# Squares of each head summed over the channels: one f32 matmul replaced by two fp32r matmuls on a rounded part and a remainder

## What is computed

```
def _head_rms(h, w):                                   # A and C
    hn = h * lax.rsqrt(jnp.mean(jnp.square(h), -1, keepdims=True) + LN_EPS)
def _head_ln(h, w):                                    # B
    hc = h - jnp.mean(h, -1, keepdims=True)
    hn = hc * lax.rsqrt(jnp.mean(jnp.square(hc), -1, keepdims=True) + LN_EPS)
```

## Time and profile before

| | us |
|---|---|
| median of three runs | 1552.47 (1551.88 to 1554.76) |
| the profiled execution | 1555.45 |
| its span, first to last instruction | 1553.7 |
| TensorE matmuls busy | 1505.2 (97%) |
| VectorE, GpSimd, ScalarE busy | 990.2, 962.1, 665.6 |
| mean granted TensorE clock | 0.989 |

### The profile page before, as it was taken

One profiled execution on the slowest core, in us unless ns is written; L12 is line 12 of the kernel. 1 busy time (PEld: TensorE's weight loads), 2 busy tenths in 40 slices (PEclk: granted clock), 3 DMA queues, 4 the chain that ended last, 5 costly groups with the idle time before them and its releaser, 6 DMA issues.

```text
span 1553.7 us, 26415 instructions
## 1 busy us (share of the span) xinstructions
PE 1505.2 (97%) x10298; PEld 1452.0 (93%) x10298; DVE 990.2 (64%) x1949; ACT 665.6 (43%) x1222; POOL 962.1 (62%) x749
## 2 busy tenths in 40 slices
PE   8899999999999999999899999999999999999996
PEld 7899988998999999999899999889899999999996
DVE  3974776357876777734448747754578777777344
ACT  5534444444444544433345444434444445444333
POOL 7666545555456667777767565544545566777774
PEclk9999999999999999999999999999999999999998
DMA  8343453444544444444434335434344344444542
GB/s 283 113 134 122 142 179 113 163 129 134 169 150 162 138 136 150 150 150 150 136 110 134 120 101 198 146 125 137 124 154 165 124 153 135 149 148 142 159 149 75
DMA packets 66260, 223.36 MB, mean 144 GB/s; under 512 B 8024, under 2 KB 12632, under 8 KB 66136
## 3 DMA queue, kind: packets, MB, share of 16 engines
q1 hardware_dynamic: 66136, 221.67, 44.5%
HBM read 206.07 MB, written 15.58 MB: 143 GB/s over the span
## 4 chain that ended last, share of the span: by engine, by line
PE 88%; DVE 8%; issue 2%; ACT 2%; DMA 1%; SPq 0%; ACTq 0%; DVEq 0%
PE gps L1327 26%; PE gps L1329 25%; PE gps L1328 25%; PE xp L1563 2%; PE xp L1565 1%; PE xp L1507 1%; PE xp L1468 1%; DVE whi L870 1%; PE xp L1555 1%; PE xp L1478 1%; DVE zc L1007 1%; PE xp L1457 1%; DMA raw<-in_w 1%; PE gps L1457 1%; PE xp L1486 0%
## 5 line engine op out<-in xcount | busy, mean ns | idle before, releaser
L620 POOL TENSOR_TENSOR wlo<-raw,whi 128x512 fp32r<-128x512 f32 x724 | 946.3, 1330 | 573.0 <-ACT whi L641 341.8
L1327 PE MATMUL gps<-xh,whi 128*128 128x320 f32 (+1 forms) x2000 | 642.7, 321 | 20.4 <-DVE xl L852 7.4
L1329 PE MATMUL gps<-xh,wlo 128*128 128x320 f32 (+1 forms) x2000 | 623.8, 312 | 0.0
L1328 PE MATMUL gps<-xl,whi 128*128 128x320 f32 (+1 forms) x2000 | 623.7, 312 | 0.0
L641 ACT ACTIVATE whi<-raw 128x1024 fp32r<-128x1024 f32 x258 | 272.3, 1056 | 353.0 <-PE gps L1329 293.1
L1327 PEld LDWEIGHTS gps<-xh,whi 128*128 128x128 f32 x2000 | 380.0, 190 | 29.4 <-DVE zc L887 8.0
L1328 PEld LDWEIGHTS gps<-xl,whi 128*128 128x128 f32 x2000 | 381.8, 191 | 3.4 <-issue 0.4
L1329 PEld LDWEIGHTS gps<-xh,wlo 128*128 128x128 f32 x2000 | 380.9, 190 | 0.0
L1327 PE MATMUL gps<-ah,whi 128*128 128x320 f32 x640 | 199.2, 311 | 0.5 <-DVE al L937 0.3
L1328 PE MATMUL gps<-al,whi 128*128 128x320 f32 x640 | 197.8, 309 | 0.0
L1329 PE MATMUL gps<-ah,wlo 128*128 128x320 f32 x640 | 197.8, 309 | 0.0
(11 more groups left out here) (307 smaller groups left out, 1846.0 us busy)
## 6 DMA issues: line engine op xcount, KB each, us to landing
raw<-in_w SPq DMA_DIRECT2D x362, 512.0 KB, 3.5
s<-in_st SPq DMA_DIRECT2D x24, 512.0 KB, 4.5
out_ss<-s SPq DMA_DIRECT2D x24, 512.0 KB, 2.7
con<-in_cst SPq DMA_DIRECT2D x4, 462.0 KB, 5.0
out_sp<-pst SPq DMA_DIRECT2D x24, 64.0 KB, 2.6
mix<-in_x SPq DMA_DIRECT2D x4, 320.0 KB, 4.8
out_y<-mix SPq DMA_DIRECT2D x8, 160.0 KB, 1.9
ee<-in_cst SPq DMA_DIRECT2D x1, 224.0 KB, 3.8
```

Of the source, the lines that this page charges most:

```text
L620: nc.gpsimd.tensor_tensor(wlo[:, c % RING, half, :], raw[:, c % RING, half, :], whi[:, c % RING, half, :].bitcast(F32), ALU.subtract).then ...
L1327: M(out, hi, xhi, start=start, stop=False)
L1328: M(out, hi, xlo, start=False, stop=False)
L1329: return M(out, lo, xhi, start=False, stop=stop)
```

## The change

ScalarE now squares `hh` into PSUM (`xp[3]`, whose content is no longer needed) and copies this, rounded, into a new fp32r tile `squares[:, 0]`. VectorE takes the remainder to `squares[:, 1]` in a phase of its own, added to `num` of C, to `a_sq` and to `b_mean`. TensorE sums both with two fp32r matmuls into the same bank. `fin` waits for the remainder in place of the squares. The order of stages is the same. `ones` becomes a view of an fp32r tile `unit`, and `seen` a view of the first 128 columns of `sq`.

```diff
-    "numC": (... ("act", (2, ("fin", -1, 3))), ("dve", 2)),
+    "numC": (... ("act", (2, ("fin", -1, 3))), ("dve", 2), ("dve", 3)),
-    "a_sq": (("act", ("num", 0, 4)), ("dve", ("num", 0, 2))),
+    "a_sq": (("act", ("num", 0, 4)), ("dve", ("num", 0, 2)), ("dve", 0)),
-    "b_mean": (("pe", ("num", 0, 3)), ("dve", 0), ("act", 1)),
+    "b_mean": (("pe", ("num", 0, 3)), ("dve", 0), ("act", 1), ("dve", 2)),
-    "finC": (("pe", (("num", 0, 3), ("num", 0, 4))), ...
-    "finA": (("pe", (("a_sq", 0, 0), ("a_sq", 0, 1))), ...
-    "finB": (("pe", (("b_mean", 0, 2), ("num", 0, 4))), ...
+    "finC": (("pe", (("num", 0, 4), ("num", 0, 5))), ...
+    "finA": (("pe", (("a_sq", 0, 1), ("a_sq", 0, 2))), ...
+    "finB": (("pe", (("b_mean", 0, 3), ("num", 0, 4))), ...
-        seen = sb("seen", [P, P])
-        ones = sb("ones", [P, 2, P])
+        unit = sb("unit", [P, 2, P], F32R)
+        ones = unit[:, :, :].bitcast(F32)
+        squares = sb("squares", [P, 2, T], F32R)
+        seen = sq[:, 0:P]
+            def square():
+                link(nc.scalar.activation(xp[3][:, 0:T], hh[:, :], ACT.Square))
+                return nc.scalar.activation(squares[:, 0, :], xp[3][:, 0:T], ACT.Copy)
...
-                        nc.scalar.activation(sq[:, :], xp[3][:, 0:T], ACT.Square)
-                        done(nc.scalar.activation(hh[:, :], xp[3][:, 0:T], ACT.Copy))
+                        link(nc.scalar.activation(hh[:, :], xp[3][:, 0:T], ACT.Copy))
+                        done(square())
                 elif stage in ("a_sq", "b_mean"):
-                    done(nc.scalar.activation(sq[:, :], hh[:, :], ACT.Square))
+                    done(square())
+                elif (stage, n, k) in (("num", "C", 5), ("a_sq", "A", 2), ("b_mean", "B", 3)):
+                    done(V.tensor_tensor(squares[:, 1, :], xp[3][:, 0:T], squares[:, 0, :].bitcast(F32), ALU.subtract))
-                    done(M(xp[4][:, 0:T], ones[:, 0, :], sq[:, :], start=True, stop=True))
+                    M(xp[4][:, 0:T], unit[:, 0, :], squares[:, 0, :], start=True, stop=False)
+                    done(M(xp[4][:, 0:T], unit[:, 0, :], squares[:, 1, :], start=False, stop=True))
```

More of the change, by code:

```diff
@@ L182 @@
     "b_score": (("pe", ("b_rope", 0, 1)), ("dve", 0)),
-    "numC": (("pe", ("fin", -1, 2)), ("act", 0), ("pe", ("fin", -1, 1)), ("act", (2, ("fin", -1, 3))), ("dve", 2)),
+    "numC": (("pe", ("fin", -1, 2)), ("act", 0), ("pe", ("fin", -1, 1)), ("act", (2, ("fin", -1, 3))), ("dve", 2), ("dve", 3)),
     "numA": (("pe", (("a_score", 0, 1), ("fin", -1, 2))), ("act", 0), ("pe", ("a_score", 0, 3)), ("act", 2), ("dve", 3)),
-    "a_sq": (("act", ("num", 0, 4)), ("dve", ("num", 0, 2))),
+    "a_sq": (("act", ("num", 0, 4)), ("dve", ("num", 0, 2)), ("dve", 0)),
     "numB": (("pe", (("b_rope", 0, 1), ("fin", -1, 2))), ("act", 0), ("pe", ("b_score", 0, 1)),
              ("act", (2, ("fin", -1, 3))), ("dve", 2)),
-    "b_mean": (("pe", ("num", 0, 3)), ("dve", 0), ("act", 1)),
-    "finC": (("pe", (("num", 0, 3), ("num", 0, 4))), ("dve", 0), ("act", (0, ("fin", -1, 3))), ("dve", 2)),
-    "finA": (("pe", (("a_sq", 0, 0), ("a_sq", 0, 1))), ("dve", 0), ("act", (0, ("fin", -1, 3))), ("dve", 2)),
-    "finB": (("pe", (("b_mean", 0, 2), ("num", 0, 4))), ("dve", 0), ("act", (0, ("fin", -1, 3))), ("dve", 2)),
+    "b_mean": (("pe", ("num", 0, 3)), ("dve", 0), ("act", 1), ("dve", 2)),
+    "finC": (("pe", (("num", 0, 4), ("num", 0, 5))), ("dve", 0), ("act", (0, ("fin", -1, 3))), ("dve", 2)),
+    "finA": (("pe", (("a_sq", 0, 1), ("a_sq", 0, 2))), ("dve", 0), ("act", (0, ("fin", -1, 3))), ("dve", 2)),
+    "finB": (("pe", (("b_mean", 0, 3), ("num", 0, 4))), ("dve", 0), ("act", (0, ("fin", -1, 3))), ("dve", 2)),
     "conv": (("dve", BEFORE),),
```

## The result

The changed kernel took 1559.23 us, the median of five runs (1558.28 to 1560.01), against 1552.47 for the kernel before, five runs too (1551.44 to 1556.25). The ratio is 1.0038, 95% interval 1.0023 to 1.0052, which is 5.9 us. Measured a second time, with 11 runs of it and 22 of the kernel before, the ratio was 1.0027 (1.0018 to 1.0036), 4.2 us. So it is slower, by 0.2 to 0.5%. The forecast was 1.0026. The time of 1559.2 us lies within the 8-in-10 range (1552.5 to 1562.0) and 0.7 us above the forecast's own range (1555.3 to 1558.5). The two profiled executions differ by 2.8 us (1558.28 and 1555.45), which lies at the low end.

What follows compares the result with a forecast made beforehand. TensorE, 97% busy, was taken to bound the kernel; -5.9 + 6.4 + 1.7 + 0.2 + 1.6 = +4.0 us on 1552.47 gave 1556.5 us, own range 1555.3 to 1558.5, 8-in-10 range 1552.5 to 1562.0.

Steps and rivals of the forecast that it cites:

- Part 2: Eight B heads: the longer chain of squares makes TensorE wait ahead of fin, 0.80 us a head, 6.4 us.
- Rival 2: The B wait is hidden, so the kernel gets faster, 1548.5 us if wholly hidden; chance 0.08.
- Part 3: A heads: the remainder delays fin 0.42 us in A0 and A3, 1.7 us in all; A1 and A2 no cost.
- Part 4: C heads: two more activations, hidden in C0 to C2; C3 pays 0.12 us, twice, 0.2 us in all.
- Part 1: Sum of squares on TensorE: two fp32r matmuls replace one f32, 0.25 us less a head, 5.9 us over 24.
- Part 5: TensorE clock: falls behind all four A waits instead of three, 1.6 us more; none behind B waits.
- rival 1: The clock falls behind the B waits too, 1.6 us each, typically two to four falls, 1561 us; chance 0.14.
- Rival 4: Two fp32r passes are no cheaper than the f32 one, +9.9 us, 1562.4 us; chance 0.05.
- Rival 3: Waits cost as forecast and no clock falls more, +2.4 us, 1554.9 us, no measurable change; chance 0.25.
- the rule I gave: Within 0.2%: rival 3, the forecast's part under 3.1 us and half of rival 2; slower: forecast, rivals 1 and 4.
- B1's L870: VectorE's rounding of a weight slot in B1, moved 1.4 us later behind the remainder; claimed covered, at no cost.
- The text on the weight load: Skill's fast weight load for non-FP32 input: would shorten the first fp32r load 0.09 us a head; left out.

Runs made afterwards that it cites:

- passes alone: Kernel before, squares written straight to fp32r and summed in two fp32r matmuls, no remainder and no added wait: 1548.43 against 1555.43 us, ratio 0.9956.
- the last experiment: Changed kernel with TensorE waiting only ahead of the sum, B's remainder behind d_split, A's small product moved from fin to num: 1550.17 us, ratio 0.9964 against before.
- the late wait: Changed kernel, but TensorE waits for the remainder only ahead of the two fp32r matmuls: 1551.78 us, ratio 0.9982 against the kernel before.

## Why the prediction was right, and where only its sum was

The sign and the time came out within the 8-in-10 range, 1556.5 forecast and 1559.2 measured. The difference, +4.0, agrees with the larger comparison (+3.6 or +4.2) better than with the first (+5.9 by the ratio, 3.6 to 8.1). The terms did not all come out. Two errors of opposite sign, 1.6 to 1.9 us and 1.6, cancelled, so that the sum fits this closely is luck; that the waits of B outweigh the gain is not.

**Part 2, B, right.** Forecast 0.80 us a head, 0.72 for the later start of `fin` and 0.08 for its loads. From VectorE's subtraction to `fin` it is now 0.69 us longer (383.24 to 384.76, against 384.75 to 385.58), and the four matmuls take 0.71 in place of 0.60. As an interval this is 0.77 (28.89 less 28.12), in eight heads alike: 6.2 us for 6.4. The sign I gave, some 0.7 us of idle time, stands in the profile as 0.53, because a dense matmul's record lasts 0.31 us where the stream advances by 0.15. Putting B back removes it. Rival 2, a hidden wait, would have needed under 0.5.

**Part 3, A0 and A3, right.** Forecast 0.42 each; the table has 0.40 to 0.42 (31.00 less 30.60). The remainder took the place behind the weighing, beside the earlier trace rows:

```profile
258.93 0.68 DVE L1120 TENSOR_TENSOR vm<-va,own 64x512 f32<-64x512 f32 x1
259.53 0.48 DVE L1098 TENSOR_TENSOR squares<-xp,squares 128x320 fp32r<-128x320 f32 x1
259.93 1.00 DVE L935 TENSOR_TENSOR mix<-gps,zc 128x320 f32<-128x320 f32 x2
...
260.10 0.68 PE L1564 MATMUL xp<-vw,kt 128*128 128x129 f32 x4 [1.61 <-DVE squares L1098]
```

**Part 4, C3, right.** Forecast 0.12; 14.96 less 14.83 is 0.13.

**Part 1, the gain, too large.** I multiplied by all 24 heads and had 5.9 us. The piece was right (0.49) and so, to some hundredths, was the gain a head where it arrives (0.22 in B, 0.25 in C3), but in six heads it doesn't reach the end: A1 and A2 (table, A2 and A3: before and passes alone are alike), and C3, behind which the fastest C3-to-A0 interval of before, 57.13 us, isn't beaten by passes alone (57.19). So 18 x 0.22 = 4.0, or 4.3 with 0.25 in the ten that aren't B. The step that failed is "on the path": I let each of the 24 sums be on it, because the chain showed it there, and didn't ask what would be late next in each stretch, as I did for the added work. In A1 it is VectorE. The timelines around A1's `fin` follow, first of the kernel before, then of the one after. L1526 (L1535 after) is the first matmul of A2's `a_score`:

```profile
293.54 2.51 POOL L620 TENSOR_TENSOR wlo<-raw,whi 128x512 fp32r<-128x512 f32 x2 [1.34 <-ACT whi L641]
...
294.91 0.29 DVE L1124 COPY pst<-xp 128x128 f32<-128x128 f32 x1 [8.93 <-PE xp L1565]
...
295.18 0.89 DVE L1127 TENSOR_TENSOR nou<-n0s,dec 128x8 f32<-128x8 f32 x1
...
298.39 0.19 PEld L1526 LDWEIGHTS xp<-capr,sel 128*128 128x128 f32 x1 [0.24 <-DVE s L1132]
```

```profile
291.90 2.53 POOL L622 TENSOR_TENSOR wlo<-raw,whi 128x512 fp32r<-128x512 f32 x2 [1.33 <-ACT whi L643]
...
293.04 0.29 DVE L1133 COPY pst<-xp 128x128 f32<-128x128 f32 x1 [3.02 <-PE xp L1575]
...
293.31 1.15 DVE L1136 TENSOR_TENSOR nou<-n0s,dec 128x8 f32<-128x8 f32 x1
...
294.58 2.15 DVE L1141 SCALAR_TENSOR_TENSOR s<-s,dec,xp 128x128 f32<-128x128 f32 x8
...
296.78 0.47 PE L1535 MATMUL xp<-capr,sel 128*128 128x448 f32 x1 [0.22 <-DVE s L1141]
```

VectorE's product of 8 columns ends at 296.07 before and 294.46 after, each time where GpSimd's pair ends (296.05, 294.43). Started earlier against GpSimd, it only gets longer (0.89 to 1.15 us). And the row before the change already told it: the weight load of L1526 waited 0.24 us for VectorE's `s`, so a saving of TensorE's ahead of it arrives only if VectorE comes earlier too. With the product moved away, VectorE of the last experiment goes straight through:

```profile
293.36 0.15 DVE L1142 COPY nou<-xp 128x1 f32<-128x1 f32 x1
...
293.43 0.15 DVE L1143 TENSOR_TENSOR nou<-nou,xp 128x8 f32<-128x8 f32 x1
293.50 2.15 DVE L1147 SCALAR_TENSOR_TENSOR s<-s,dec,xp 128x128 f32<-128x128 f32 x8
```

There the first matmul of `a_score` no longer waits and costs 0.20 us in the chain, in place of 0.46 before. That experiment shows it for A1 and A2. For C3 I have only the absence of a gain.

**Part 5, the clock, wrong.** I added 1.6 us for a fourth fall behind the A waits, and net the clock added nothing. Stretches of the kernel after (us, busy PE, PEld, DVE, ACT, POOL, PEclk, DMA share, GB/s), beside the earlier trace rows:

```profile
59.30:62.70 3.40, 3.40 (x15) 3.40 (x15) 2.78 (x4) 1.73 (x4) 2.77 (x3) 0.51 0.20 31
352.90:356.30 3.40, 3.40 (x15) 3.40 (x14) 3.09 (x13) 1.00 (x2) 1.12 (x1) 0.50 0.00 0
1001.60:1005.00 3.40, 3.40 (x14) 3.40 (x14) 1.38 (x3) 2.14 (x5) 3.40 (x4) 0.52 0.27 59
1032.40:1039.20 6.80, 6.80 (x28) 5.97 (x28) 3.78 (x15) 1.00 (x2) 1.08 (x1) 0.52 0.05 19
1124.50:1128.00 3.50, 3.13 (x22) 2.64 (x22) 2.77 (x8) 0.78 (x2) 2.15 (x2) 1.00 0.00 0
413.00:417.00 4.00, 3.47 (x24) 2.84 (x24) 3.78 (x9) 2.91 (x7) 1.32 (x2) 1.00 0.00 0
```

The A waits grew from 1.2 or 1.3 to 1.6 or 1.7 us, and behind that of A3 in layer 1 (1124.5) the clock now stays at its upper level of 2.4 GHz; behind that of A0 (1032.4) it stays at 1.2 GHz for 6.8 us, twice as long as before. Counted in stretches of 3.4 us the bodies of both kernels hold five falls in the first traces, and four each in the second; I leave out the lower clock between the layers, which every trace has. The mean granted clock of all runs of the second comparison is 0.990 for both kernels. By place, the two traces of the kernel before have three each behind A waits and two and one behind C (at 220 and 988 us), which I hadn't counted; those of the changed kernel have three and four behind A, one and none behind C, and one at 59 us. So a fourth behind A came in one of two traces, and as many were missing elsewhere. The stretch from which I argued that a wait does no harm, 56 to 60 us, is followed by the lower clock in the first trace of the changed kernel (59.3), and not in its second. No fall stands behind a B wait (413 to 417) in any trace, so rival 1 is out. Net of all terms: -4.0 + 6.2 + 1.6 + 0.2 = +4.0 us, or +3.7 with the larger gain.

**Rival 4** is refuted by the passes alone. **Rival 3** (+2.4, no further fall) had the clock right and the gain wrong.

**The chances.** By the rule I gave, within 0.2% adds up to 0.36 and faster by more to 0.04; the text has 0.34 and 0.06.

**A cover that was thinner than I said.** I called B1's L870, 1.4 us later, covered. That held for this kernel only because TensorE waited too. With the late wait it cost 0.7 us a layer.

The text on the weight load stands: the first fp32r load takes 186 ns in the trace of after (L1574), no faster than f32.

## What to carry to other kernels

When an operand is made by a longer chain, move its wait down to the instruction that reads it; the same additions cost 4.2 us with the wait ahead of the whole phase and gained 2.8 with it ahead of the sum. Read slack for each instance (here 24 heads in five kinds of place), for the gains as well as for the costs: a gain on the bounding engine ends where another engine's wait takes over. A wait on a busy engine also needs a look at what stands behind it in program order, since a stage with no part in the change (`d_split`) paid for it.

## What was not expected of the hardware

An operation of VectorE with two SBUF inputs of 8 columns took 0.154 to 0.901 us in the kernel before (L1127, median 0.526) and 0.158 to 1.158 in the one after; placed where GpSimd's weight pass had no hold on it, it took 0.156 to 0.159 in all eight heads. In A1, where both ran, it ended 0.02 to 0.03 us behind GpSimd's instruction, before the change and after. The Trainium skill (SBUF — State Buffer, section "Terms", "shared port pair") says that VectorE and GpSimd take a pair of SBUF ports in turn, for a whole instruction. These numbers agree.

The clock fell behind waits of 1.2 us and stayed up behind one of 1.7 us, in kernels that differ little. I can't say from these traces which wait is followed by a fall, so I would price one as a part of the range and not of the sum.
